# Moving low parts and dot products between stages of a hybrid decoder block with expert retrieval: 24 low parts made early instead of 18

## The reference

```python
q = (xf @ w_query).reshape(t, 8, 2, 128)
scores = einsum('thpk,hpnk->thpn', q, sub_keys)            # 128 keys for each half
v1, i1 = top_k(scores[:, :, 0], 16); v2, i2 = top_k(scores[:, :, 1], 16)
best, pos = top_k(v1[..., :, None] + v2[..., None, :], 16)  # 16 of 256 pairs
e1 = i1 at pos // 16; e2 = i2 at pos % 16
experts = e1 * 128 + e2                                     # 8 heads x 16 = 128 of 16384 a token
gates = softmax(best)
a = gelu(einsum('cd,ced->ce', x, expert_u[experts])) * gates
out = einsum('ce,ced->cd', a, expert_v[experts])
```

## Time and profile before

| | us |
|---|---|
| median of 3 runs | 1590.77 |
| fastest, slowest | 1590.66, 1591.87 |
| the profiled execution's own time | 1593.7 |
| its span in the profile | 1591.6 |
| TensorE busy in the span | 1582.0 (99%) |
| VectorE busy | 1289.7 (81%) |
| ScalarE busy | 701.9 (44%) |
| GpSimd busy | 455.4 (29%) |

### The profile page before, as it was taken

The page is one execution under the profiler, slowest core; times in us unless marked ns, Lnnn a source line. Parts: engine busy times, 40 slices in busy tenths (PEclk is TensorE's granted clock), DMA queues, the critical chain, the costliest instruction groups (busy, mean ns, idle before and its releaser), DMA issues.

```text
span 1591.6 us, 25557 instructions
## 1 busy us (share of the span) xinstructions
PE 1582.0 (99%) x8606; PEld 1400.8 (88%) x8606; DVE 1289.7 (81%) x2395; ACT 701.9 (44%) x937; POOL 455.4 (29%) x390
## 2 busy tenths in 40 slices
PE   9999999999999999999999999999999999999998
PEld 8888888888888999999999999998888888888886
DVE  6967833335478899987899998789998999999997
ACT  5444533333333433343676776433334333333334
POOL 1011100000000011155434323434452565555451
PEclk9999999999999999999999999999999999999999
DMA  6477732322322698899999999999999999999994
GB/s 215 147 247 238 237 106 93 105 92 95 117 80 89 199 327 294 272 295 321 380 407 406 417 390 372 405 368 379 387 413 360 390 414 412 413 414 409 410 372 168
DMA packets 151840, 463.75 MB, mean 291 GB/s; under 512 B 16772, under 2 KB 47546, under 8 KB 150114
## 3 DMA queue, kind: packets, MB, share of 16 engines
q1 hardware_dynamic: 82080, 230.64, 39.4%
q0 software_dynamic: 49344, 176.91, 29.2%
q10 hardware_dynamic: 20354, 55.51, 9.5%
HBM read 407.07 MB, written 55.93 MB: 291 GB/s over the span
## 4 chain that ended last, share of the span: by engine, by line
PE 90%; DMA 4%; DVE 2%; issue 2%; ACT 1%; POOL 0%; SPq 0%; DVEq 0%; ACTq 0%; POOLq 0%
PE bank L1060 18%; PE bank L1062 18%; PE bank L1061 17%; PE bank L1248 11%; PE bank L1250 11%; PE bank L1249 11%; PE bank L1214 3%; DMA rows<-u_rows,expert 3%; PE bank L1126 1%; DVE w_lo L1301 1%; DMA rows<-u_rows,expert_extra 1%; DVE rows L1709 1%; DMA h_t<-x_t 1%; ACT w_hi L710 0%; POOL rows L617 0%
## 5 line engine op out<-in xcount | busy, mean ns | idle before, releaser
L710 ACT ACTIVATE w_hi<-w_raw 128x1024 fp32r<-128x1024 f32 x347 | 366.2, 1056 | 327.3 <-PE bank L1250 215.6
L1060 PE MATMUL bank<-xn_hi,w_hi 128*128 128x344 f32 (+1 forms) x1472 | 506.4, 344 | 2.0 <-DVE w_lo L1301 1.9
L1301 DVE TENSOR_TENSOR w_lo<-w_raw,w_hi 128x1024 fp32r<-128x1024 f32 x329 | 401.3, 1220 | 127.7 <-ACT w_hi L710 126.3
L1062 PE MATMUL bank<-xn_hi,w_lo 128*128 128x344 f32 (+1 forms) x1472 | 503.7, 342 | 0.0
L1061 PE MATMUL bank<-xn_lo,w_hi 128*128 128x344 f32 (+1 forms) x1472 | 499.7, 339 | 0.0
L617 POOL DMA_INDIRECT rows<-u_rows,expert x128 | 159.9, 1249 | 624.3 <-PE bank L1062 372.1
L1248 PE MATMUL bank<-w_hi,a_hi 128*128 128x512 f32 x768 | 298.9, 389 | 0.0
L1250 PE MATMUL bank<-w_hi,a_lo 128*128 128x512 f32 x768 | 298.8, 389 | 0.0
L1249 PE MATMUL bank<-w_lo,a_hi 128*128 128x512 f32 x768 | 298.8, 389 | 0.0
L1060 PEld LDWEIGHTS bank<-xn_hi,w_hi 128*128 128x128 f32 x1472 | 276.2, 188 | 19.9 <-DVE w_lo L1301 2.6
L1061 PEld LDWEIGHTS bank<-xn_lo,w_hi 128*128 128x128 f32 x1472 | 277.3, 188 | 17.3 <-issue 0.2
(11 more groups left out here) (243 smaller groups left out, 1508.8 us busy)
## 6 DMA issues: line engine op xcount, KB each, us to landing
w_raw<-u SPq DMA_DIRECT2D x128, 512.0 KB, 6.0
w_raw<-v SPq DMA_DIRECT2D x128, 512.0 KB, 7.2
g_dram<-g_sb ACTq DMA_DIRECT2D x12, 2048.0 KB, 10.8
g_in<-g_dram SPq DMA_DIRECT2D x84, 256.0 KB, 9.5
act_dram<-act_out ACTq DMA_DIRECT2D x54, 344.0 KB, 7.2
act_in<-act_dram SPq DMA_DIRECT2D x54, 344.0 KB, 9.0
w_raw<-gate SPq DMA_DIRECT2D x32, 512.0 KB, 3.3
w_raw<-w_in SPq DMA_DIRECT2D x31, 512.0 KB, 3.7
```

What stands on the lines that cost most here:

```text
L710: act.activation(w_hi[:, slot, :], w_raw[:, slot, :], ACT.Copy).then_inc(hi_done, 1)
L1060: pe.matmul(out, hi, x_hi, start=k == 0, stop=False)
L1062: last = pe.matmul(out, lo, x_hi, start=False, stop=k == NB - 1)
L1301: dve.tensor_tensor(w_lo[:, slot, :], w_raw[:, slot, :], w_hi[:, slot, :].bitcast(F32), ALU.subtract).then_inc(lo_done, 1)
```

## The change

Four things are changed together.

1. **Early low parts.** 24 in place of 18, in four buffers instead of three, so the groups 1 to 12 of the u stage have early tiles instead of 1 to 9 (u tiles 41, 43, 45, 47, 49 and 51 are new). Each of the iterations 2 to 7 of the projections makes four. `early_hi` moves into `scratch`. GpSimd issues store k, and then the load for buffer k - 1, where it used to issue store k, wait for its landing, and reload the same buffer.
2. **Dots and low parts in the retrieval.** 15 dots instead of 10 up to `expert_last`, with other tables for the low parts; one more u tile (48) has its turn before it.
3. **Dots behind it.** 18 instead of 20 in `DOTS_BEFORE` (which now starts at n = 45), 24 instead of 28 in `DOTS_PLAIN`; one more is left for the v stage. The extra rows are rows 24 to 63 instead of 17 to 56. The exponentials come one tile later.
4. **Loads of x.** The 16 loads of `x_behind`, which were issued ahead of 16 successive gathers, are issued ahead of every second gather (first 8) and then of 8 successive ones, beginning at row 19 instead of row 14. The store of the extra dots comes 4 tiles later in its round.

```diff
-EARLY_STEPS = 9
+EARLY_STEPS = 12
-EARLY_BUFFERS = 3
+EARLY_BUFFERS = 4
...
-QUERY_SPLITS = (..., (1, 1, 1, 1, 1, 0, 0), (1, 1, 1, 1, 1, 0, 0))
-QUERY_DECODES = ((0, 1), (0, 1), (1, 1), (1, 1))
+QUERY_SPLITS = (..., (1, 1, 1, 1, 1, 0, 0), (2, 0, 1, 1, 1, 0, 0))
+QUERY_DECODES = ((0, 1), (0, 1), (2, 0), (2, 0))
...
-DOTS_SEARCH = (1, 1, 1, 2)
-DOTS_DECODE = (1, 1, 1, 1)
-BEFORE_FIRST = 44
+DOTS_SEARCH = (1, 2, 2, 2)
+DOTS_DECODE = (1, 2, 2, 2)
+BEFORE_FIRST = 45
-DOTS_BEFORE = (1, 1, 1, 2, 1, 2, 1, 1, 2, 1, 1, 1, 1, 1, 2, 1)
+DOTS_BEFORE = (1, 1, 1, 1, 1, 1, 1, 2, 1, 1, 1, 1, 2, 2, 1)
-DOTS_PLAIN = (2, 2, 1, 2)
+DOTS_PLAIN = (2, 1, 1, 2)
-EXTRA_FIRST = DOTS_TOPK + 7
+EXTRA_FIRST = DOTS_TOPK + 9
+X_BEHIND = (tuple(EXTRA_SHOWN + 1 + 2 * k for k in range(SHARED)) +
+            tuple(EXTRA_SHOWN + 2 * SHARED + k for k in range(SHARED)))
...
-        early_hi = early("early_hi", [P, D], F32R)
+        early_hi = MemoryMap(nc, scratch_at)("early_hi", [P, D], F32R)
...
                 store_early(k)
-                if k + EARLY_BUFFERS < N_EARLY:
-                    pool.wait_ge(early_stored[k % EARLY_BUFFERS], 16 * (k // EARLY_BUFFERS + 1))
-                    load_early(k + EARLY_BUFFERS)
+                if 1 <= k and k - 1 + EARLY_BUFFERS < N_EARLY:
+                    pool.wait_ge(early_stored[(k - 1) % EARLY_BUFFERS], 16 * ((k - 1) // EARLY_BUFFERS + 1))
+                    load_early(k - 1 + EARLY_BUFFERS)
...
-                if EXTRA_SHOWN < q <= EXTRA_SHOWN + (X_BUFFERS - X_BESIDE) * SHARED:
-                    load_extra(X_BESIDE * SHARED + q - EXTRA_SHOWN - 1)
+                if q in X_BEHIND:
+                    load_extra(X_BESIDE * SHARED + X_BEHIND.index(q))
...
-            g_round(ROUNDS - 3, midway=store_extra, after=2)
+            g_round(ROUNDS - 3, midway=store_extra, after=SLOTS + 2)
```

More of the change, by code:

```diff
@@ L1185, in _ @@
                     u_tile(step, b, early=b in EARLY_TILES)
-            with pe.Fori(EARLY_STEPS + 1, TURN_AT) as step:
-                for b in range(SLOTS):
-                    u_tile(step, b)
+            assert EARLY_STEPS + 1 == TURN_AT
             pe.wait_ge(x_last_ready, 2)
@@ L1414, in conv_block @@
                 chain.did(dve.tensor_tensor(z_pad[:, TAPS - 1:], bank[2][:], c_sb[:], ALU.mult))
+                if not raw:
+                    early_rest(i, 1)
                 split_weight(SLOTS * i + 6, 2)
@@ L1450, in in_block @@
                 conv_low(i)
[L1451 removed]
+                early_rest(i, 3)
             def scaled_p(i):
```

26 lines of the change are left out of this document (12 added, 14 removed).

## The result

| | before | changed |
|---|---|---|
| median of 6 runs each, us | 1590.88 | 1596.12 |
| fastest, slowest | 1589.71, 1592.26 | 1595.67, 1597.13 |
| the profiled execution's own time | 1593.7 | 1595.67 |
| its span in the profile | 1591.6 | 1593.9 |

The changed kernel takes 1.003 of the time before, with a 95% interval of 1.002 to 1.0041: 5.2 us slower. The prediction was 1588.3, with a range of 1586.6 to 1592.0, so it was wrong in sign and the range did not hold the time. (The ratios in this text weigh means of executions, the times are medians; the two can differ by up to 0.1%.)

What follows compares the result with a forecast made beforehand. TensorE was taken as the bound, busy 1582.0 of 1591.6 us. Savings of 3.7 + 0.2 less 0.2 gave 3.7 us in the profile, taken as 2.5 for timed runs: 1588.3, range 1586.6 to 1592.0.

Steps and rivals of the forecast that it cites:

- The low part of tile 57: U stage: VectorE ends it at 734.2, 4.0 us ahead of TensorE's need at 738.22, where it was 2.07 late.
- The wait for `mix_lo`: End of the projections: TensorE's wait grows from 0.5 to 0.7 us, a cost of 0.2.
- The fourth buffer's load: Projections: issued at 181.8, landed by 188.4, 0.6 us before ACT wants it; cost 0.
- the rival with early low parts that land late: Tiles 49 and 51: `w_lo` lands over 12 us, TensorE waits; 1595.9, chance 0.12.
- The retrieval's five dots more: Up to `expert_last`: VectorE gets 2.5 us more work in one more tile's 3.77; cost 0.
- the signs named for "right": No wait at u tile 57, clock 1.00 at 740 to 760 us, `mix_lo` wait 0.7, plain tiles' row waits below 15.
- those for "wrong": Waits on `lo_loaded` at tiles 45 to 51, `mix_lo` over 1.5, clock below 1.00, or span falling 3.7 without the median.
- The main gain: U tile 57: removing TensorE's late start, 2.07, and slower clock, 1.64, saves 3.7 us profiled; 2.5 taken for timed runs.
- The plain tiles: 985 to 1052 us: 24 dots instead of 28 remove TensorE's second wait for a low part, saving 0.2 us.
- the first rival: Timed runs have little of the tile 57 wait, or extra rows move it to a later tile; 1590.4, chance 0.13.
- GpSimd's spread loads of x: Loads of x ahead of gathers: spreading them costs nothing on any path and only makes gathers earlier.
- slower: Outcome of a time slower by more than measurement can tell, about 0.2% or 3.2 us; chance 0.12.

Runs made afterwards that it cites:

- early low parts alone: The kernel before with the 24 early low parts in four buffers and nothing else of the change: 1591.52, before 1591.42, ratio 1.0004.
- the loads left out: The changed kernel without the eight loads of x that fill the first buffer a second time (part of the computation then wrong): 1589.64, before 1590.92.
- the best variants: The changed kernel with two dots fewer (n = 57, 58) and loads of x ahead of successive gathers, 1589.63; or without eight loads of x, 1589.64.
- the last kernel above: The kernel before with 24 dots in the plain tiles and the first extra row at row 24 instead of 17: 1591.08, before 1590.75.
- the changed kernel again: The changed kernel, unaltered, run and profiled once more on another chip: 1596.60, before 1590.71, ratio 1.0034.
- the variant with two dots earlier: The changed kernel with two dots made at n = 50 and 51 instead of n = 57 and 58: 1593.70, before 1591.23, ratio 1.0013.

## Why the prediction was wrong, step by step

**Its steps ahead of the masks were right.** The low part of tile 57 was to end at 734.2 with 4.0 us in hand; it began at 733.38, so ended at 734.60, 3.7 in hand:

```profile
733.38 1.22 DVE L1299 TENSOR_TENSOR w_lo<-w_raw,w_hi 128x1024 fp32r<-128x1024 f32 x1
```

The wait for `mix_lo` is 0.7, as put, against the 0.5 of the earlier trace rows. The fourth buffer's load was issued at 181.75 (181.8), and ScalarE made that high part at 189.00, as put from the earlier trace rows. No early low part came late, which clears the rival with early low parts that land late; "early low parts alone" says the same in time. The retrieval's five dots more brought no wait. All the signs named for "right" are there, and of those for "wrong" only the clock below 1.00: the signs looked at the places that the sum looked at. One small step was counted twice: the landings of the earlier trace rows run from the start of the gather's issue, so the issue of 1.76 is already in them, and the rows 22 and 23 had 3.4 us in hand at the median and were 1.9 late at the longest, not 1.6 and 3.7. It changed no term.

**The main gain, 3.7 us taken as 2.5, is the first term that failed.** It was read from one execution. The prediction saw the sign of it, the median 2.9 under that execution, and then took "somewhat above the middle". The runs show about nothing: the wait at tile 57 comes in one of seven profiles, and in none of 23 timed runs that would show it. That the three timed runs lay 1.2 apart was taken as that wait; the plain tiles' waits are what varies.

**The plain tiles, 0.2 us, were under-sized by five.** The working from the earlier trace rows had the direction right (28 dots fall behind, 24 hardly), but its price was not of this place. The second wait of 0.2 in the earlier trace rows lies at the start of the kernel, in the projections,

```profile
15.36 0.50 PE L1060 MATMUL bank<-u_hi,w_hi 128*128 128x512 f32 x1 [0.18 <-DVE w_lo L1301]
```

and it is still there, at 15.38, with 24 dots. In the plain tiles the profile of before has no wait of TensorE at all, while other executions with 28 dots wait there up to 2.3 us. Worth 1.0 and 1.1 by runs. In the changed kernel the same waits are

```profile
DVE rows L1709 <- DMA rows<-u_rows,expert: 12.4, 10, 3.2
```

below the 15 that was named. This is the part of the change that pays.

**The loss came from a step that is not there.** "From row 24 on each extra gather still takes 7.9 us" stands in the first rival, and the price put on it was only the lost gain, 1590.4. The slack of u tiles was followed, never that of the masks, which VectorE makes in the same queue, and which had 0.98 us in the trace of before: the cost of VectorE's later work behind tile 57 was put at nothing without a reason, and the changed kernel waits 4.2 us for masks, with 1.5 of slower clock behind. Three parts of the change then draw on it:

| part, alone in the kernel before | us, by medians |
|---|---|
| early low parts | +0.1 |
| extra rows seven later | +1.0, and +1.3 where both have 24 dots in the plain tiles |
| one dot more at n = 57 | +3.3 |
| loads of x spread | +1.9 |
| 24 dots in the plain tiles | -1.1, -1.0 |

With the mean of the pairs the sum is 0.1 + 1.2 + 3.3 + 1.9 - 1.1 = 5.4; the changed kernel is 5.2 and 5.9 above. The intervals of the ratios are 1.3 to 2.3 us either way, and those of the early low parts and of the later rows against the kernel before reach below zero. That the parts add up so well is luck in good part, since taking them out of the changed kernel again gives back other amounts than each cost (2.3 for the dot, about 4.3 for the spread loads, about 7 for two dots or for the loads left out).

"GpSimd's spread loads of x cost nothing on any path, they only make gathers earlier" was the second failed sentence. It looked at the rows where the loads were taken away, not at those where they were put, and there they doubled with the reloads. The order of instructions alone shows that. And 18 dots for 20 read as a relief; but the three dots taken away (n = 44, 47 and 49) stood ahead of n = 53, where VectorE of the changed kernel idles 5.7 us for ScalarE anyway, and one was added behind it, at n = 57, from where to 812 us it never idles for ScalarE.

Of the rivals, the right one was the first (the extra rows' waits move), with its sign wrong; no case on the slower side named the masks, and "slower" had 0.12. That the case with late early low parts came out at 1595.9, next to the measured 1596.1, is a coincidence: none of its waits occurred.

**What stays open.** Summed over TensorE's starts from 700 to 1055 us, waits and slower clock cost 6.5 us in the profile of the changed kernel, and its timed median lies 6.5 above the best variants' 1589.6: there the profile stands for the timed runs. In the profile of the kernel before the sum is 4.1 us, and its timed median is only 1.3 above those variants. Recording alone doesn't bring the wait at tile 57, since the six other profiles with the same place of the extra rows lack it; what did in that one execution isn't known. Whether the loads of x cost by their issue, by their traffic or by both is open, and so is why single rows took 14 to 15 us to land. The wait for `a_lo` near 1575 us (1.4 us in the last kernel above, 1.5 in the second profile of the changed one, 0.4 or less in the others) stays unexplained. The parts in the retrieval were not tried alone.

## What to carry to other kernels

List every product of an in-order engine that the bound engine waits for, and read the slack of each one from the trace before you move work on it: here the low parts had 4 us and the masks 1, and both come out of the same queue. Slack is rebuilt at once only where the engine idles for something else (from mask to mask it grew by 0.4 us here); work moved from ahead of such an idle place to behind it can cost more than its own duration (3.3 us for a dot of 1.23 here). A wait of one profiled execution may be missing in most others; where the median lies below that execution by nearly as much, as here, doubt it first. And look up where in the kernel a wait lies before it prices a term.

## What the runs showed of the hardware that was not expected

The clock did not follow the length of the wait. In stretches of 20 us it was 0.91 around or behind waits of 1.90 (before), 2.49 (the last kernel above) and 3.46 us, and 0.83 around one of 3.63 (the changed kernel again), but stood at 1.00 around one of 2.70 and one of 2.97, both between 804 and 808 us, as the 2.49 was. The stretch of the variant with two dots earlier, with its 2.70:

```profile
800.00:820.00 20.00, 17.30 (x151) 16.89 (x150) 16.47 (x24) 11.96 (x15) 5.10 (x5) 1.00 0.97 368
```

So the 1.64 us that the prediction added for the slower clock is a cost that comes in some executions only.

Gathered rows also took longer to land once the rounds had begun: in the kernel before the landing times (min, median, max, from the start of the issue) of the tile `rows` are, from 741 to 812 us,

```profile
DMA to landing us min/median/max: 7.1/9.6/11.5
```

where the earlier trace rows, from 540 to 760 us, had a median of 7.9. A slot's round is 1.2 us from the end of its dot to the next gather, with one load of x ahead, 9.6 to landing and 1.2 of the dot: 12.0 us for four rows, an estimate from these medians. What is put ahead of a gather comes on top, and so does a landing of 14 to 15 us.

The Trainium skill ("Trainium Kernel Development and Optimization", Key Constraints) says that issuing from several engines only saves issue time, since all run on the same 16 DMA engines. No run here issued the loads of x from another engine. The DMA share is 0.99 to 1.03 from 760 to 820 us in the changed kernel. Leaving eight of them out, with their issue and their traffic, was worth 6.5 to 7.2 us at the end.
